# The MoE router reads the raw residual, and rstd is applied to its logits

## The reference, cut to what matters

```python
def rmsnorm(x, g):
    y = x * lax.rsqrt(jnp.mean(x * x, axis=-1, keepdims=True) + NORM_EPS)
    return y * g
def modulate(h, shift, scale):
    return h * (1.0 + scale) + shift

h = modulate(rmsnorm(x, norm_ffn[i]), mod[:, 3], mod[:, 4])   # per layer
scores = sigmoid(h @ w_router)            # (T, 16)
sel = scores + b_router
# best group of 4 by the sum of its two best, then the 2 best experts in it
# combine = scores of the picked two, normalised to sum 1
hid = silu(x @ wg[e]) * (x @ wu[e]) * combine;  y = hid @ wd[e]
```

## Time and profile before

| what | value |
|---|---|
| median of 3 runs | 1330.68 us (1322.2, 1330.95, 1330.68) |
| the profiled execution's own time | 1324.39 us |
| its span in the profile | 1322.7 us |
| TensorE busy | 1200.5 us, 91% |
| VectorE / ScalarE / GpSimd busy | 383.4 / 316.7 / 122.6 us |
| memory traffic | 389.57 MB, mean 295 GB/s |
| mean granted TensorE clock | 0.962 |

### The profile page before, as it was taken

One profiled execution on the slowest core, in us unless ns is written; L12 is line 12 of the kernel. 1 busy time (PEld: TensorE's weight loads), 2 busy tenths in 40 slices (PEclk: granted clock), 3 DMA queues, 4 the chain that ended last, 5 costly groups with the idle time before them and its releaser, 6 DMA issues.

```text
span 1322.7 us, 24788 instructions
## 1 busy us (share of the span) xinstructions
PE 1200.5 (91%) x10404; PEld 697.5 (53%) x10404; DVE 383.4 (29%) x1218; ACT 316.7 (24%) x716; POOL 122.6 (9%) x188
## 2 busy tenths in 40 slices
PE   4788998789998899899978999999999997789996
PEld 2446544447885554654447643445465444565544
DVE  1345111340004522621132023341451115561113
ACT  1240111231124522211133211230411114401113
POOL 2000100210000000111020000000002111001101
PEclk9898999889999999899989999999999998989998
DMA  9999999794326873898979223891689987658993
GB/s 349 412 421 421 409 413 421 282 350 151 119 96 247 298 314 140 321 409 347 412 271 351 69 96 106 357 363 64 251 344 357 419 359 277 273 214 355 397 390 136
DMA packets 89708, 389.57 MB, mean 295 GB/s; under 512 B 10456, under 2 KB 38604, under 8 KB 53240
## 3 DMA queue, kind: packets, MB, share of 16 engines
q1 hardware_dynamic: 71568, 336.61, 65.2%
q0 software_dynamic: 17456, 51.07, 10.5%
q10 hardware_dynamic: 568, 0.23, 0.1%
HBM read 370.96 MB, written 27.96 MB: 302 GB/s over the span
## 4 chain that ended last, share of the span: by engine, by line
PE 76%; DMA 10%; DVE 5%; SPq 3%; issue 3%; ACT 2%; POOL 1%; POOLq 0%; DVEq 0%; ACTq 0%
PE bank L491 70%; DMA sb_ring<-in_w_ada 3%; PE bank L966 3%; SPq L449 2%; DMA slot_out<-sb_arena,sb_homes 2%; DMA sb_arena<-slot_out,sb_slots 2%; DMA sb_ring<-in_w_exp_up 2%; POOL sb_arena L2132 1%; DVE sb_xT L1994 1%; PE bank L984 1%; DMA slot_out<-sb_arena 1%; DMA sb_arena<-token_rows,sb_rows 1%; PE bank L894 0%; DVE sb_arena L1954 0%; PE bank L1017 0%
## 5 line engine op out<-in xcount | busy, mean ns | idle before, releaser
L491 PE MATMUL bank<-sb_ring,sb_arena 128*32 128x256 f32 (+1 forms) x6112 | 449.9, 429 | 17.3 <-DMA sb_ring<-in_w_exp_down 8.0
L491 PEld LDWEIGHTS bank<-sb_ring,sb_arena 128*32 128x32 f32 x6112 | 212.5, 111 | 197.8 <-issue 108.0
L491 PE MATMUL bank<-sb_arena 128*128 128x128 f32 (+11 forms) x776 | 140.7, 361 | 10.9 <-DVE sb_arena L1840 7.0
L491 PE MATMUL bank<-sb_ring,sb_hT 128*128 128x256 f32 x624 | 140.8, 387 | 6.2 <-ACT sb_hT L1225 6.2
L491 PEld LDWEIGHTS bank<-sb_ring,sb_hT 128*128 128x128 f32 x624 | 120.6, 194 | 26.9 <-issue 9.1
L491 PEld LDWEIGHTS bank<-sb_arena 128*128 128x128 f32 (+2 forms) x776 | 102.7, 194 | 45.6 <-issue 13.0
L491 PE MATMUL bank<-sb_ring,sb_cond 128*2 128x512 f32 x768 | 94.9, 616 | 8.8 <-DMA sb_ring<-in_w_ada 8.5
L491 PE MATMUL bank<-sb_arena,sb_ring 128*128 128x384 f32 (+2 forms) x288 | 95.5, 507 | 3.0 <-DVE sb_arena L1710 2.1
L1941 DVE TENSOR_TENSOR sb_arena<-sb_arena,bank 128x256 f32<-128x256 f32 x40 | 16.8, 421 | 248.9 <-PE bank L491 248.9
L491 PE MATMUL bank<-sb_hT,sb_ring 128*128 128x384 f32 x256 | 85.8, 498 | 2.6 <-ACT sb_hT L1225 2.6
L491 PEld LDWEIGHTS bank<-sb_arena,sb_ring 128*128 128x128 f32 (+1 forms) x288 | 49.9, 181 | 44.9 <-issue 19.0
(11 more groups left out here) (318 smaller groups left out, 1013.8 us busy)
## 6 DMA issues: line engine op xcount, KB each, us to landing
sb_ring<-in_w_ada SPq DMA_DIRECT2D x96, 1024.0 KB, 8.7
sb_ring<-in_w_exp_gate SPq DMA_DIRECT2D x60, 1024.0 KB, 10.4
sb_ring<-in_w_exp_up SPq DMA_DIRECT2D x60, 1024.0 KB, 12.7
sb_ring<-in_w_exp_down SPq DMA_DIRECT2D x60, 1024.0 KB, 15.1
sb_ring<-in_w_mlstm_in SPq DMA_DIRECT2D x12, 1024.0 KB, 12.1
token_rows<-sb_arena POOLq DMA_DIRECT2D x12, 512.0 KB, 7.6
slot_out<-sb_arena POOLq DMA_DIRECT2D x9, 512.0 KB, 8.8
sb_scratch<-in_w_exp_gate SPq DMA_DIRECT2D x4, 1024.0 KB, 9.0
```

The lines of the kernel that those rows point to most:

```text
L491: return pe.matmul(out, lhsT, rhs, start=first, stop=last)
```

## The change

What it does:

- `w_ra` (new) holds gain * w_router, for context and latent tokens side by side: 32 stationary columns. VectorE makes it in two instructions (`router_weights`). In layers 1 to 3 they stand ahead of the residual, in layer 0 behind it.
- `shift_logits`: TensorE multiplies the shift column by `w_rt`, 16 matmuls (8 chunks, two kinds of token) with one stationary column and 16 moving ones, all on output partition 0. VectorE copies the row (`shift_copy`). Three matmuls with one contraction row add it to the logits.
- `raw_logits`: 8 matmuls of `w_ra` by `xT` on bank 5, interleaved with the square sums in layers 1 to 3, behind them in layer 0.
- VectorE multiplies these sums by rstd as it copies them, three `fold` matmuls turn them, and the picks begin.
- VectorE's 16 instructions on `hT` become 8 without the gain (`scale_input`): 4 ahead of the picks, 4 behind them. Gain and shift are put on by ScalarE (`modulate`), 2 instructions ahead of the Exp and 14 behind it, all ahead of the `htok` copies.
- TensorE turns the first half of all tokens' channels, then counts the picks (5 matmuls in place of 9), then turns the second half. `ada(g, 4, 5, 6)` come behind all of that; `ada(g, 0..3)` now stand behind the logits.
- GpSimd's stores wait for copies 4, 5 and 6 of 6, where they waited for 2, 4 and 6.
- Several semaphores are merged; in the mLSTM, waits on `state_in` now count four transfers.

```diff
+TURNS = [0, 2, 4, 1, 3, 5]
...
+            def raw_logits(L, n, a, b):
+                pe.wait_ge(wra_ready, L + 1)
+                for k in range(a, b):
+                    pe.wait_ge(x_ready, 8 * n + k + 1)
+                    q = k % 4
+                    ins = mm(ps[5][32 * q:32 * q + 32, 0:TOK], w_ra[:, k, :, :].rearrange("p c e -> p (c e)"), xT[:, k, :],
+                             k < 4, k >= 4)
+                    if k >= 4:
+                        ins.then_inc(lg_full, 1)
+
+            def shift_logits(L, bank):
+                pe.wait_ge(mod_added, 3 * L + 2)
+                for c in range(2):
+                    for k in range(KC):
+                        ins = mm(bank[0:1, c * NE:(c + 1) * NE], mod[:, L, 24 + k, c:c + 1], w_rt[:, k, :], k == 0, k == KC - 1)
+                ins.then_inc(sr_full, 1)
+
+            def norm_routed(L, n):
+                if L == 0:
+                    norm(n)
+                    ada(2, 6, 7)
+                    ada_columns(2)
+                    shift_logits(0, ps[5])
+                    raw_logits(L, n, 0, KC)
+                else:
+                    for a, b in ((0, 2), (2, 4), (4, 6), (6, 7), (7, 8)):
+                        raw_logits(L, n, a, b)
+                        norm_squares(n, a, b)
+                    norm_mean(n)
+                pe.wait_ge(sr_ready, L + 1)
+                for t in range(NT):
+                    c = min(t, 1)
+                    mm(ps[4][:, t * NE:(t + 1) * NE], ones[0:1, :], shift_row[:, c * NE:(c + 1) * NE], t == 0, False)
+                pe.wait_ge(lg_ready, L + 1 + (L > 0))
+                for t in range(NT):
+                    c = min(t, 1)
+                    ins = mm(ps[4][:, t * NE:(t + 1) * NE], lg[:, t * P:(t + 1) * P], fold[:, c * NE:(c + 1) * NE], False, t == NT - 1)
+                ins.then_inc(rt_full, 1)
...
             def pool_mixer(r):
+                if r:
+                    shift_logits(3, ps[7])
...
                 turn_head(MH - 1)
                 pe.wait_ge(hsT_ready, 8)
                 pe.wait_ge(n_copied, 1)
+                shift_logits(1, ps[5])
                 project(r, lambda k: (qT if k % 2 == 0 else kT)[:, k // 2, :], hsT_ready, [8] * KC)
...
             def mla(r):
+                shift_logits(2, ps[7])
...
             def experts(L, n):
-                side(ps[6], w_rt, n)
-                for c in range(2 * NT):
-                    if c == 2:
-                        unfold(ps[6], L + 1 + (L > 0), rt_full)
+                def count_picks():
+                    pe.wait_ge(mask_ready, L + 1)
+                    ...
+                for c in TURNS:
+                    if c == 1:
+                        count_picks()
+                    pe.wait_ge(h_ready, 16 * n + (8 if c % 2 == 0 else 16))
+                    if c == 4:
+                        pe.wait_ge(rt_e, L + 1)
                     for k in range(4):
                         ins = pe.transpose(ps[c][:, k * P:(k + 1) * P], ...)
                     ins.then_inc(ht_full, 1)
                 for g in ADA_WINDOW[L]:
-                    ada(g, 4, 5)
-                pe.wait_ge(mask_ready, L + 1)
-                ...
-                for g in ADA_WINDOW[L]:
-                    ada(g, 6)
+                    ada(g, 4, 5, 6)
...
+            def modulate(L, n, a, b):
+                gain, bias = amp[:, L, 1, :, :], mod[:, L, 24:32, :]
+                for k in range(a, b):
+                    act.wait_ge(h_scaled, 16 * n + 2 * k + 2)
+                    for c in range(2):
+                        o = h_out(k, c)
+                        act.activation(o, o, ACT.Identity, bias=bias[:, k, c:c + 1], scale=gain[:, k, c:c + 1]).then_inc(h_ready, 1)
...
             def experts(L, n):
+                modulate(L, n, 0, 1)
                 act.wait_ge(rt_full, L + 1)
-                act.activation(rt[:, 1, :], ps[6][:, 0:48], ACT.Exp, scale=-1.0).then_inc(rt_e, 1)
+                act.activation(rt[:, 1, :], ps[4][:, 0:48], ACT.Exp, scale=-1.0).then_inc(rt_e, 1)
+                modulate(L, n, 1, KC)
...
+            def router_weights(L):
+                for c in range(2):
+                    ins = v.tensor_tensor(w_ra[:, :, c, :], w_rt[:, :, :], amp[:, L, 1, :, c:c + 1].to_broadcast([P, KC, NE]), ALU.mult)
+                ins.then_inc(wra_ready, 1)
+
+            def scale_input(a, b):
+                for k in range(a, b):
+                    v.tensor_tensor(hT[:, k, :], xT[:, k, :], rstd[:, :], ALU.mult).then_inc(h_scaled, 2)
+
+            def norm_routed(L, n):
+                v.wait_ge(lg_full, 4 * (L + 1 + (L > 0)))
+                v.wait_ge(rstd_ready, n + 1)
+                v.tensor_tensor(lg, ps[5][:, 0:TOK], rstd[:, :], ALU.mult).then_inc(lg_ready, 1)
+                scale_input(0, KC // 2)
...
                 v.tensor_tensor(by4(pick), by4(pick), gb.unsqueeze(2).to_broadcast([P, 12, 4]), ALU.mult).then_inc(mask_ready, 1)
+                scale_input(KC // 2, KC)
                 v.wait_ge(mask_ready, L + 1)
```

More of the change, by code:

```diff
@@ L527, in ada_beside, with norm_squares @@
                         ada_columns(groups[i])
-            def norm(n):
-                for k in range(KC):
+            def norm_squares(n, a, b):
+                for k in range(a, b):
                     if k % 2 == 0 or k == KC - 1:
@@ L2035, in _ @@
                 norm(2 * L, amp[:, L, 0, :, :])
+                if L > 1:
+                    shift_copy(L, ps[7])
                 if kind == 0:
@@ L2041, in _ @@
                     mla(2 * L)
+                if L == 1:
+                    shift_copy(L, ps[5])
+                if L:
+                    router_weights(L)
                 residual(2 * L, gpool[:, L // 3, :, :] if kind == 0 else mod[:, L, 16:24, :], lambda c: ps[c % 4], 8 * L)
@@ L2046, in _ @@
                     mod_columns(2)
-                norm(2 * L + 1, amp[:, L, 1, :, :])
+                    shift_copy(L, ps[5])
+                    router_weights(0)
+                norm_routed(L, 2 * L + 1)
                 experts(L, 2 * L + 1)
@@ L2155, in _ @@
             g.memset(vx[:, :, :, DV:VX], 1.0).then_inc(pool_set, 1)
-            g.dma_start(mask[:, :, :], A["k_mask"]).then_inc(tables_in, 16)
-            g.dma_start(sel, A["k_sel"]).then_inc(tables_in, 16)
+            g.dma_start(mask[:, :, :], A["k_mask"]).then_inc(state_in, 16)
+            g.dma_start(sel, A["k_sel"]).then_inc(state_in, 16)
             for d in range(2):
```

94 lines of the change are left out of this document (50 added, 44 removed).

## The result

The changed kernel takes 1339.53 us (median of 20 runs, 1328.38 to 1344.41), the kernel before in the same comparison 1322.7 (20 runs, 1317.62 to 1332.44). The ratio is 1.0107, with a 95% interval of 1.009 to 1.0124: some 14 us slower by this ratio (the two medians lie 16.8 us apart). I had forecast -2.6. The profiled execution has a span of 1335.4 us where the kernel before had 1322.7, and a mean granted clock of 0.954 for 0.962.

A forecast was written before the change was run, and what follows sets the result against it. It took layer 0 as bound by transfers and layers 1 to 3 by one serial chain from rstd to the gather. Layer 0 at 0 and +1.1, -1.6, -2.1 us for the others gave -2.6, so 1328.1 us, range 1316 to 1336.

The forecast's parts named there:

- The failed step: Layer 0: GpSimd's token stores move to copies 4, 5, 6; the gather, 8.8 to 9.2 us long, covers them.
- Layer 0 at 0, ±1.1: Layer 0: bytes due by 206 us are unchanged and loads cover TensorE's gain, so 0, with 1.1 us either way.
- The raw products: Ahead of rstd: eight `raw_logits` products and eight square sums take six steps, 4.1 us; four steps would be 2.8.
- R: The moment when rstd is ready; forecast later by 2.2 us in layer 1 and by 1.8 in layers 2 and 3.
- `shift_logits`: 16 one-column products, 32 records at 0.07: 2.3 us, all counting in layer 1, with 0.8 to 4.1 as ends.
- The picks: Routing stage: the picks are ready at R + 7.5 us, where they were at R + 13.5 before.
- VectorE's scalings: Scalings of 384 columns at 0.5 us each: four ahead of the picks take 2.0, four late ones 2.0.
- `modulate`: ScalarE behind the picks: 0.71 us a chunk, 5.68/8, so `hT` is complete 3.4 us behind the picks.
- The gather: Starts at R + 15.1 us in layers 1 and 2, R + 14.0 in layer 3; gains of 3.4 and 4.4.
- The added products are nearly free: Rival: quadrants stay full and the one-column products cost 0.8 us; 1321.6 to 1322.7 us, chance 0.25.
- The change doesn't shorten the chain: Rival: TensorE's queue alone holds the gather in layers 1 to 3, so earlier logits do nothing; 1339.3 us, chance 0.03.
- a transfer enters the chain in layers 1 to 3: Sign that would show the forecast wrong: a transfer appearing in the chain of waits of layers 1 to 3.

The follow-up runs named there:

- h2: The kernel before, with GpSimd's three stores of token rows in layer 0 alone held until VectorE has the slots of round 0; ratio 1.0072 against the kernel before.
- g1: The changed kernel, with SyncE's weight loads of layers 1 and 2 from the fifth expert unit on held until the token stores landed; 1.0067 against the kernel before.

## Why the prediction was wrong, by its steps

- **The failed step** is the sentence that GpSimd's stores move from copies 2, 4 and 6 to 4, 5 and 6, with "which covers the stores". I costed the move at nothing and named the gather as its cover, without a subtraction. The traces' subtraction: in layer 0 the last store had 16.0 us until the row numbers and took 14.1 to land, so 1.9 us were left over, and the change issues it 5.3 us later and has the row numbers 1.6 us earlier. In layers 1 and 2 some 5 us were left over; the store goes out 3.1 and 2.8 us later and the row numbers come 3.6 and 4.7 earlier, and in layer 2 the landing grew from 10.2 to 16.2 us. The fetch waits for the store in all three. The forecast itself made the cover shorter, by an earlier gather, and I used the old length, which at 8.8 to 9.2 us was less than the landing in layers 0 to 2 even so.
- **Layer 0 at 0, ±1.1.** It was +8.4. Of these 1.8 lie ahead of rstd; h2, which alters nothing there, shows 1.6 of them too, so they aren't the change's. Behind rstd it is +6.6, and h2 makes +7.0 of the stores alone. I had read "bound by transfers" as "TensorE's delays are free". They were not free where they delayed a transfer of their own; 341 GB/s for 403 followed.
- **The raw products.** I took six steps, 4.1 us, as the order in the source meets quadrants it has just used. Measured: 2.8, my "four full steps". R came later by 1.0, 0.6 and 0.6, where I had 2.2, 1.8 and 1.8.
- **`shift_logits`.** 2.3 us taken, 0.95 measured: 0.03 for a record. The Trainium skill's rule (page "TensorEngine Tiling (Array Packing)", section "Instruction Overhead"), 60 cycles a matmul and with it, as an estimate, 0.8 us, is near this trace; my "row with the smallest moving part" was the worse guide. The low end of 0.8 that I took didn't follow from the row I named for it, which gives 0.02 a record.
- **The picks** at R + 7.5: 7.3. **VectorE's scalings** at 0.5: 1.95/4 = 0.49. Both right.
- **`modulate`** at 0.71 a chunk, from instructions with one added column. With scale and bias columns a chunk takes 3.61/4 = 0.90, and a half 3.61 for 2.84. The copies ended 15.0, 14.3 and 14.9 us behind rstd, not 14.0; in layers 1 and 3 the turns ahead of them ran at half speed too.
- **The gather** at R + 15.1, 15.1 and 14.0: 17.2, 15.6 and 15.1. In layer 1 the turns ran at half speed (2.82 us for 1.53 in layer 2, the same 12 records), which is most of the 2.1.
- **What I hadn't seen at all** is a gain: the gather's 60 records take 6.86 us for 9.17. Without it each layer's gather would be some 2 us longer. But the low clock went to other stretches, and over the whole span there is more of it.
- **The rivals.** "The added products are nearly free" was right in its mechanism. "The change doesn't shorten the chain" gave 1339.3, close to the measured 1339.5, by luck: it adds 8.6 us to my three runs' median of 1330.68, while 20 runs of the kernel before have 1322.7, and its cause is refuted by the trace, where the mask is 6 us earlier. None of my cases held a late transfer of tokens, though my list of what would make me wrong did ("a transfer enters the chain in layers 1 to 3").

## What to carry to other kernels

When a step is moved, list the transfers it issues, and give each its slack as a subtraction: issue to first use, less the landing time, with both ends at their new places. A chain that gets shorter takes slack from everything issued at its old pace beside it. And a stage that is bound by transfers isn't a place where delays are free: whatever starts a transfer or frees its buffer is on the path there.

## What the runs showed of the hardware

- The last of three stores of 512 KB from GpSimd's queue lands in 3.8 to 6.4 us where few or no weight loads run beside it (layer 3, and layers 1 and 2 of g1), and in 9.3 to 16.2 us where loads of 1 MB start on SyncE's queue beside it (layer 2 of the changed kernel: four of them within 9.5 us). The Trainium skill (page "DMA: Bandwidth & Descriptors", section "Queues, rings and completion order") says that each DMA engine takes turns between queues packet by packet. By that alone, as an estimate, three stores beside one loading queue would need about twice their time alone, some 8 to 13 us; layer 1 agrees with its 9.3, layers 0 and 2 with 15.1 and 16.2 don't. The same section says that a completion signal lands only after earlier writes of its engine across queues, which would let a store wait for loads that were queued with it. No run here separates the two.
- Sixteen float32 products with 32 stationary columns (32 records) ran as four full steps though the source pairs them by twos: the rows show raw, squares, raw, squares in groups of 8 records, in 2.8 us. How that order comes about no run shows.
- TensorE's slow stretch moved. Before, the gather ran at a granted clock of 0.73 to 0.77. With the shorter stage the low clock (0.64) falls on the turns ahead of it, 1161 to 1174, where TensorE is busy for 6.9 of 13 us, and the gather has 1.00. It isn't free there: the turns take 2.82 us for 1.53. And with each long wait for tokens comes a stretch at 0.50 of its own (122.5 to 132.7 and 983 to 996 us).
- ScalarE's instruction with a scale and a bias column took 483 ns for 128 columns and 586 for 256; with the bias column alone it took 388 and 495.
